# One attention's heads between its projection tiles, and a linear attention in chunk pairs with one scan

## What is computed

```python
a_val, a_gate, q, k, v, b_gate = jnp.split(h @ w_in, EVEN_SPLITS, axis=-1)
q = apply_rope(rmsnorm(to_heads(q, N_Q_HEADS), q_norm_g[li]), cos, sin)   # 6 heads of 128
k = apply_rope(rmsnorm(to_heads(k, N_KV_HEADS), k_norm_g[li]), cos, sin)  # 2 heads of 128
ck = rmsnorm(to_heads(ck, N_KV_HEADS), k_norm_g[li])                      # 256 context tokens
k_all = jnp.concatenate([ck, k], axis=1)
```

## Time and profile before

| | us |
|---|---|
| Runs | 2109.66, 2120.30, 2115.14 |
| Median | 2115.14 |
| The profiled execution's own time | 2111.56 |
| Its span | 2109.7 |
| Its mean granted clock of TensorE | 0.968 |

### The profile page before, as it was taken

How to read it: one execution, slowest core, us unless ns; L and a number is a source line. 1 busy time by engine, 2 the same in 40 slices (tenths; PEclk the granted TensorE clock), 3 DMA queues, 4 the chain that set the end, 5 groups by cost and what they waited for, 6 DMA issues and landing times.

```text
span 2109.7 us, 26132 instructions
## 1 busy us (share of the span) xinstructions
PE 1984.3 (94%) x9634; PEld 1528.7 (72%) x9634; DVE 1165.4 (55%) x1908; ACT 822.2 (39%) x1381; POOL 121.0 (6%) x118
## 2 busy tenths in 40 slices
PE   7997998999799989999999999998999999999997
PEld 5784556788466567776888888775777688888775
DVE  5765756996587686565674234225464574323323
ACT  3424442443422334545543234224445554323321
POOL 0004000000200011000310000000000040000000
PEclk8998899999999999998999999999999899999998
DMA  8583008677001262111212222232211121222222
GB/s 323 189 309 138 0 1 296 239 271 267 16 8 65 95 245 100 41 61 41 81 61 97 95 88 99 80 104 93 83 56 45 41 101 57 94 91 98 99 80 80
DMA packets 46943, 233.38 MB, mean 111 GB/s; under 512 B 5095, under 2 KB 6631, under 8 KB 29832
## 3 DMA queue, kind: packets, MB, share of 16 engines
q1 hardware_dynamic: 46856, 232.22, 30.7%
HBM read 229.97 MB, written 2.10 MB: 110 GB/s over the span
## 4 chain that ended last, share of the span: by engine, by line
PE 80%; DVE 9%; ACT 4%; DMA 3%; issue 2%; POOL 1%; SPq 1%; DVEq 0%; POOLq 0%; ACTq 0%
PE banks L2050 14%; PE banks L2052 14%; PE banks L2051 14%; PE banks L2271 4%; PE banks L2368 3%; PE banks L2370 3%; PE banks L2369 3%; DMA w_raw<-in_wt 2%; PE banks L2291 2%; PE banks L2203 1%; PE banks L2401 1%; PE banks L2214 1%; DVE mod_raw L1278 1%; PE banks L2092 1%; PE banks L2413 1%
## 5 line engine op out<-in xcount | busy, mean ns | idle before, releaser
L1263 DVE TENSOR_TENSOR w_low<-w_raw,w_high 128x1024 fp32r<-128x1024 f32 x184 | 224.8, 1222 | 275.7 <-ACT w_high L506 275.4
L2050 PE MATMUL banks<-h_high,w_high 128*128 128x512 f32 x904 | 352.8, 390 | 7.6 <-DVE w_low L1263 3.9
L2051 PE MATMUL banks<-h_low,w_high 128*128 128x512 f32 x904 | 351.8, 389 | 0.0
L2052 PE MATMUL banks<-h_high,w_low 128*128 128x512 f32 x904 | 351.8, 389 | 0.0
L506 ACT ACTIVATE w_high<-w_raw 128x1024 fp32r<-128x1024 f32 x184 | 193.6, 1053 | 181.9 <-PE banks L2052 140.5
L2050 PE MATMUL banks<-hidden_high,w_high 128*128 128x512 f32 x512 | 207.2, 405 | 0.0
L2050 PEld LDWEIGHTS banks<-h_high,w_high 128*128 128x128 f32 x904 | 169.8, 188 | 46.9 <-issue 9.6
L2052 PE MATMUL banks<-hidden_high,w_low 128*128 128x512 f32 x512 | 200.2, 391 | 0.0
L2051 PE MATMUL banks<-hidden_low,w_high 128*128 128x512 f32 x512 | 200.0, 391 | 0.0
L2052 PEld LDWEIGHTS banks<-h_high,w_low 128*128 128x128 f32 x904 | 169.7, 188 | 35.3
L2051 PEld LDWEIGHTS banks<-h_low,w_high 128*128 128x128 f32 x904 | 169.8, 188 | 34.8
(11 more groups left out here) (495 smaller groups left out, 3551.5 us busy)
## 6 DMA issues: line engine op xcount, KB each, us to landing
w_raw<-in_wt SPq DMA_DIRECT2D x129, 1024.0 KB, 4.9
mod_raw<-in_wmod SPq DMA_DIRECT2D x132, 512.0 KB, 5.0
mod_first<-in_wmod SPq DMA_DIRECT2D x12, 512.0 KB, 14.0
cmp_w<-in_cmp_w SPq DMA_DIRECT2D x2, 2048.0 KB, 8.7
x<-in_xT SPq DMA_DIRECT2D x1, 2048.0 KB, 13.2
dft<-in_dft SPq DMA_DIRECT2D x1, 2048.0 KB, 12.8
out_x<-x SPq DMA_DIRECT2D x8, 256.0 KB, 2.0
hy_w<-in_hy_w SPq DMA_DIRECT2D x8, 192.0 KB, 3.3
```

The lines of the kernel that those rows point to most:

```text
L1263: v.tensor_tensor(low[:, :, :].rearrange("p k c -> p (k c)"), RAW[b // 2][:, b % 2, :], high[:, :, :].rearrange("p k c -> p (k c)").bitcas ...
L2050: mm(out, high[:, k, :], H[:, kk, :], start=start and k == 0, stop=False)
L2051: mm(out, high[:, k, :], L[:, kk, :], start=False, stop=False)
L2052: last = mm(out, low[:, k, :], H[:, kk, :], start=False, stop=stop and k == KT - 1)
```

## The change

**First attention.** The loop over tiles 4 to 19 is written out. `HEADS_AT` says at which tile a head is begun: two at tiles 4 and 5, one at each of 6 to 11. At tile t, ACT takes the root of the heads of tile t-1 and squares those of tile t; PE, after the tile's own 24 matmuls, sums the heads of t and rotates those of t-1; DVE makes the sine part and output of the heads of t-2, then `w_low` of the next tile, then gain and cosine of the heads of t-1, then the tile's units. The heads' sums go to banks 4 and 5 and the rotations to 6 and 7; their buffers are two each. The value transposes stand behind scores 0 and 1. The pool mixer waits for 12 tiles taken and for head 9.

**Linear attention.** Two chunks lie on the two halves of the partitions. So there are 4 groups of transposes, `GA` is 128x4x256 (and the mask is loaded twice), and each chunk's products go to a bank by the chunk's parity. A state's product is four small ones, one for each head, of 32 by 64, so that all states stand in two banks; DVE copies them to `GKV` as [value channel, chunk], and one scan with the decays in `GD` gives all states `GS`, with the chunk innermost. The queries are spread over four buffers `GQ`, one for each head and zero elsewhere (POOL clears them), so that a product reads all 128 rows of `GS`.

**Order behind tile 23.** PE: two groups of transposes, sums of conv, two groups, states, sums of gmlp, results, sums of nsa, the attention's own. ACT and DVE take each group's squares, logarithm, exponential, highs and lows by itself, and `EARLY` has the order conv, gmlp, nsa. The squares of conv move to tile 22; the attention's squares have buffers of their own (`GSQ`). The sums of group 2 stand ahead of tile 3 instead of tile 2, and behind its wait for `w_low`.

```diff
+    GS = at(BIG_AT + 12 * 2 * KB, [P, 64, 8], name="gla_state")
+    GKV = at(BIG_AT + 2 * 2 * KB, [P, 64, 8], name="gla_new")
+    GD = at(BIG_AT + 6 * 2 * KB, [P, 64, 8], name="gla_decays")
+    GA = at(BIG_AT + 19 * 2 * KB, [P, 4, 256], name="gla_att")
+    GQ = [at(BIG_AT + 2 * KB * n, [P, S], name="gla_query") for n in (8, 9, 10, 21)]
+    GSQ = [at(BIG_AT + 2 * KB * n, [P, S], name="gla_sq") for n in (4, 11)]
...
-    BATCHES = (range(0, 4), range(4, NC1))
...
+    HEADS_AT = {4: (0, 1), 5: (2, 3), 6: (4,), 7: (5,), 8: (6,), 9: (7,), 10: (8,), 11: (9,)}
...
+    EARLY, LATE = (0, 1, 6, 7, 2, 3), (4, 5)
...
+    def own_place(c):
+        return slice(64 * (c % 2), 64 * (c % 2) + 64), slice(64 * (c // 2), 64 * (c // 2) + 64)
...
+            if j >= 2:
+                act.wait_ge(taken, (4 + R1[j][1] if R1[j][0] == "q" else R1[j][1]) + 1 + PRIME)
...
+        def head_root(j):
+            rs, n = RSS[j % 2], head_src(j)[1]
+            act.wait_ge(*when(f"hn_ss.{j}"))
+            if j >= 2:
+                act.wait_ge(*when(f"hn_zn.{j - 2}"))
+            nc.scalar.activation(rs[:, 0:n], bank(4 + j % 2, n), ACT.Ln, bias=EPSC[:, :], scale=1.0 / P).then_inc(*did(f"hn_ln.{j}"))
+            act.wait_ge(*when(f"hn_ln.{j}"))
+            nc.scalar.activation(rs[:, 0:n], rs[:, 0:n], ACT.Exp, scale=-0.5).then_inc(*did(f"hn_rs.{j}"))
...
+        for t in range(4, EV_IN):
+            next_tile(t // 4, t % 4)
+            for j in heads_at(t - 1):
+                head_root(j)
+            for j in heads_at(t):
+                head_square(j)
+            copy_out(t // 4, t % 4, z(t), ACT.Copy if t < 12 else ACT.Silu)
+        logs_and_exps()
...
-                nc.scalar.activation(DECY[:, :], GB[:, :].rearrange("p (c t) -> p c t", t=64)[:, :, 63], ACT.Exp, scale=1.0 / 16).then_inc(*did("gla_decay.all"))
+                nc.scalar.activation(GD[:, :, :], GB[:, :].rearrange("p (c t o) -> p o c t", t=64, o=1)[:, :, :, 63].to_broadcast([P, 64, 8]), ACT.Exp, scale=1.0 / 16).then_inc(*did("gla_decay.all"))
...
+                    group_squares(0, ("gm_var.0", "gm_var.1"))
...
             group_squares(3, ("gr_ss.0", "gr_ss.1"))
+            group_log(0)
+            group_root(0)
+            split_high(Q + 6, 1)
             group_squares(1, ("gr_ss.6", "gr_ss.7"))
-            for g in (0, 3, 1):
-                group_log(g)
-            for g in (0, 3, 1):
-                group_root(g)
-            split_high(Q + 6, 1)
-            act.wait_ge(*when("gr_n.3"))
-            for k in range(4):
-                mixed_high(k)
-            for m in range(2):
-                act.wait_ge(*when(f"gla_o.{m}"))
-                nc.scalar.activation(GO[:, m, :], bank(6 + m), ACT.Copy).then_inc(*did(f"gla_out.{m}"))
-                act.wait_ge(*when(f"gr_ss.{2 + m}"))
-                nc.scalar.activation(SQ[m][:, :], bank(6 + m), ACT.Square).then_inc(*did(f"gla_sq.{m}"))
-            for k in (6, 7):
-                mixed_high(k)
+            normal_high(0)
+            normal_high(1)
+            group_log(3)
+            group_root(3)
+            gla_result(0)
+            gla_result(1)
+            group_log(1)
+            group_root(1)
+            normal_high(6)
+            normal_high(7)
             for m in range(2):
...
+            normal_high(2)
+            normal_high(3)
             high_of(Q + 6, 2, KEPT[2][0])
-            group_squares(2, ("gla_ss.0", "gla_ss.1"))
+            group_squares(2, ("gr_ss.2", "gr_ss.3"))
             high_of(Q + 6, 3, KEPT[3][0])
             group_log(2)
             group_root(2)
-            act.wait_ge(*when("gr_n.5"))
             for k in LATE:
-                mixed_high(k)
+                normal_high(k)
...
-        pool.wait_ge(taken, EV_IN + PRIME)
-        pool.wait_ge(*when("in_tabc.all"))
+        pool.wait_ge(taken, 12 + PRIME)
+        pool.wait_ge(*when("hn_out.9"))
...
+                dve.wait_ge(*when(f"hn_zn.{j}"))
+                v.tensor_tensor(RA[j % 2][:, :], ZN[j % 2][:, :], COS0, mul).then_inc(*did(f"hn_ra.{j}"))
...
             dve.wait_ge(*when(f"hn_rot.{j}"))
-            v.tensor_tensor(RB[j % 2][:, :], bank(2 + j % 2), SIN0, mul).then_inc(*did(f"hn_rb.{j}"))
+            v.tensor_tensor(RB[j % 2][:, :], bank(6 + j % 2), SIN0, mul).then_inc(*did(f"hn_rb.{j}"))
             dve.wait_ge(*when(f"hn_rb.{j}"))
             dst = KALL[:, h, CTX:CTX + S] if kind == "k" else z(4 + h)
             v.tensor_tensor(dst, RA[j % 2][:, :], RB[j % 2][:, :], add).then_inc(*did(f"hn_out.{j}"))
...
+        for t in range(4, EV_IN):
+            q, b = t // 4, t % 4
+            if t == 16:
+                dve.wait_ge(*when("silu.row2"))
+                v.tensor_copy(CROW[:, :], CROW2[:, :]).then_inc(*did("next_cond.all"))
+                dve.wait_ge(*when("next_cond.all"))
+            for j in heads_at(t - 2):
+                head_sin(j)
+            next_tile(q, b)
+            for j in heads_at(t - 1):
+                head_norm(j)
+            for j in heads_at(t - 1):
+                head_cos(j)
+            side(q, b, split=False)
...
+                for h in range(4):
+                    rows = slice(32 * h, 32 * h + 32)
+                    v.scalar_tensor_tensor(GQ[h][rows, :], z(11, rows), 32 ** -0.5, GE[3][rows, :], mul, mul).then_inc(*did("gla_m.3" if h == 3 else f"gla_q.{h}"))
...
-                        v.tensor_copy(GS[rows, 1, cols_], bank(4)[rows, cols_]).then_inc(*did(f"gla_st.{c}.{h}"))
+                v.copy_predicated(GA[:, h, :], GMASK[:, 0:256], bank(h, 256)).then_inc(*did(f"gla_att.{h}"))
...
+            dve.wait_ge(*when("gla_kv.3"))
+            v.tensor_copy(GKV[:, :, :].rearrange("p v (j q) -> p q j v", q=2), pair_of_banks(2).rearrange("p q (j v) -> p q j v", v=64)).then_inc(*did("gla_new.all"))
+            dve.wait_ge(*when("gla_new.all"))
+            v.tensor_tensor_scan(GS[:, :, :].rearrange("p v c -> p (v c)"), GD[:, :, :].rearrange("p v c -> p (v c)"),
+                                 GKV[:, :, :].rearrange("p v c -> p (v c)"), 0.0, mul, add).then_inc(*did("gla_st.all"))
...
-            for g in (0, 3, 1):
-                group_norm(g)
+            group_norm(0)
             split_low(Q + 6, 1)
-            dve.wait_ge(*when("gla_o.1"))
-            for k in EARLY:
+            mixed_low(0)
+            mixed_low(1)
+            group_norm(3)
+            group_norm(1)
+            for k in EARLY[2:]:
                 mixed_low(k)
...
-        with led.loop(pe, "ev_in", EV_IN // 4 - 1) as i:
-            for b in range(4):
-                body(i + 1, b, "n0_lo")
...
+            mm(bank(4 + j % 2, n), ONES, SQ[j % 2][:, 0:n], start=True, stop=True).then_inc(*did(f"hn_ss.{j}"))
...
-                mm(bank(2 + j % 2), ROPE0, ZN[j % 2][:, :], start=True, stop=True).then_inc(*did(f"hn_rot.{j}"))
...
+        for t in range(4, EV_IN):
+            body(t // 4, t % 4, None)
+            for j in heads_at(t):
+                head_sum(j)
+            for j in heads_at(t - 1):
                 rot(j)
...
+            if n < 2:
+                pe.wait_ge(taken, EV_IN - 2 + 2 * n + PRIME)
...
+            if n < 2:
+                values_to_tokens(range(3 * n, 3 * n + 3))
...
-            pe.wait_ge(*when("gla_m.2"))
-            for c in range(8):
-                pe.wait_ge(*when(f"gla_tok.{c - 2}" if c >= 2 else "p2t.15"))
-                pe.sem_inc(passed, 1)
-                for m, src in enumerate((GE[2][:, :], z(13), z(14))):
-                    last = nc.tensor.transpose(bank(4 + c % 2)[0:64, m * P:(m + 1) * P], src[:, 64 * c:64 * c + 64], IDENT)
-                last.then_inc(*did(f"gla_tok_mm.{c}"))
...
-            pe.wait_ge(*when("gla_att.3"))
-            for c in range(7):
-                pe.wait_ge(*when("gla_tok.7" if c < 2 else f"gla_st.{c - 2}.3"))
-                mm(bank(4 + c % 2, 256), GV[:, c, 0:P], GV[:, c, P:3 * P], start=True, stop=True).then_inc(*did(f"gla_kv.{c}"))
-                if c:
-                    group_sum((0, 3, 1)[(c - 1) // 2], (c - 1) % 2)
...
+                for m, src in enumerate((GE[2][:, :], z(13), z(14))):
+                    last = nc.tensor.transpose(bank(4 + j % 2)[:, m * P:(m + 1) * P], src[:, P * j:P * j + P], IDENT)
+                last.then_inc(*did(f"gla_tok_mm.{j}"))
...
+                        last = mm(bank(2 + q)[32 * h:32 * h + 32, 64 * j:64 * j + 64], GV[rows, j, 32 * h:32 * h + 32], GV[rows, j, P + 64 * h:P + 64 * h + 64], start=True, stop=True)
+                last.then_inc(*did(f"gla_kv.{j}"))
...
+                    rows, own = own_place(c)
+                    b = 4 + 2 * m + c % 2
...
+                        mm(bank(b)[64 * hp:64 * hp + 64, own], GV[rows, c // 2, P + 64 * h:P + 64 * h + 64], GA[rows, h, own], start=True, stop=c == 0)
                     if c:
-                        last = mm(bank(6 + m)[:, cols_], GS[:, c, P * m:P * m + P], GE[3][:, cols_], start=False, stop=True)
+                        for hp in range(2):
```

(33 more changed lines are left out.)

193 lines of the change are left out of this document (81 added, 112 removed).

## The result

The changed kernel took 2084.01 us (median of 4 runs, 2077.00 to 2087.95), the kernel before 2112.40 beside it: ratio 0.986, 95% interval 0.9837 to 0.9882. It is faster by 28 us at the medians. I had said 2100, with 2088 to 2112 as the range: the direction was right, the size about half. The profiled execution took 2087.95 us, 23.6 less than the 2111.56 of before.

The account below looks back on a forecast made before the run. The prediction took TensorE (PE), busy 94% of the span, as the bound. 17.5 - 2 x 2 = 13.5 us off 2111.56 gave 2098.1, 2101.7 for the median, leaned to 2100 us; range 2088 to 2112.

Parts of the forecast that it names:

- the states of Part B: Linear attention on PE: 32 state matmuls of 64 columns, priced at 4.2 to 6.6 us a layer, taken as 5.0.
- Part B: Linear attention of the two layers: 3.5 us won and 5.6 lost in each, so 2 us slower per layer.
- the stall from POOL: Tiles 13 to 19: the pool mixer beside VectorE makes w_low late, 8 us in sum, bounds 0 and 18.6.
- a head's sums and rotations: Work added to PE between the in-projection tiles: 16 x 1.06 + 2 x 0.62 = 18.2 us.
- the conv sums: Layers, moved before the states: two sums on PE at half clock, 2 x 1.75 = 3.5 us.
- Part A: First attention, heads between in-projection tiles: 25.5 us before stalls, less 8 of stall, gives 17.5 us.
- The tail's term: Layers, from the end of the attention's own sums to the late parts: 17.1 us instead of 11.5.
- (1): In-projection: POOL and VectorE disturb each other little, stall 0 to 2 us, time 2094; chance 0.20.
- (2): Layers: PE keeps its full clock, 5.4 us more gained per layer, time 2091; chance 0.10.
- (3): VectorE becomes the bound: all 18.6 us of POOL fall on PE, layers at half clock, about 2119 at worst; chance 0.10.
- (5): First attention: the interleaving isn't one, as a head's rotation waits on PE for its gain; 2112; chance 0.05.
- (4): Layers' results: weight loads with a 32-byte step cost more, 112 x 0.18 = 20 us if doubled, 2120; chance 0.07.

Follow-up runs that it names:

- e1: The kernel before with only the first attention's part of the change (heads between the tiles): 2089.8 us, 0.9881 of the kernel before.
- e3: The changed kernel with the pool mixer waiting for all 20 tiles, as before the change: 2077.8 us, 0.9824 of the kernel before.
- e2: The kernel before with only the layers' (linear attention) part of the change: 2105.4 us, 0.9955 of the kernel before.
- e7: The changed kernel with the state products reordered, the four groups of one head and partition half following each other: 2090.3 us, 0.9901 of the kernel before.
- e4: The changed kernel with the sums of group 2 ahead of tile 2 again: 2077.0 us, 0.9828 of the kernel before.
- e8: The changed kernel with nsa sums between the results' halves, highs and lows early, group 2 sums ahead of tile 2: 2075.3 us, 0.9827 of the kernel before.
- e10: The changed kernel with the results' state products reading only their head's 32 rows, without the masked query buffers: 2083.1 us, 0.9853 of the kernel before.

## Why the prediction was wrong

The two parts were forecast at 17.5 - 2 x 2 = 13.5 us and gave 31.6 in the profile. Four terms of the sum were priced too high: the states of Part B (5.0 for 1.05, twice), the stall from POOL (8 for 3.8), a head's sums and rotations (18.2 for 14.6) and the conv sums (3.5 for 2.2, twice). Together that is 7.9 + 4.2 + 3.6 + 2.6 = 18.3 us, of the 18.1 that were missed.

**Part A** was forecast at 17.5 us and gave 23.9 in the profile, 25 in e1. Two terms were too large.
- The price of a head's sum or rotation. I took the 1.05 us of a sum between small products; between tiles it is 0.86 (127.40 - 126.54). Sixteen of them and two halves make 14.6 us instead of 18.2: 3.6 us.
- "Sum 8 us", the stall from POOL. It was 3.8, and e3 shows that POOL is its only cause. The step that failed is the walk through the tiles with a whole POOL product of 1.5 us between any two VectorE operations, which lets all 18.6 us of POOL fall on VectorE. The row on which I based it said 1.75 - 0.68 = 1.07 more, and the units beside POOL took 2.30 - 1.22 = 1.08 more, where the product alone takes 5.70 / 4 = 1.43; beside the product of 2.14 they took 2.96 - 1.22 = 1.74 more. Each time it is some 0.4 us less than the product, so a wait for the whole instruction, as the prediction has it, is more than these rows show. The nine units and four `w_low` from 162 to 192 us lost 13.3 us in all. The mechanism was right, the row's own number should have been used. Tile 18 was then 1.4 us late instead of 5.
- The rest: 43.4 - 14.6 - 3.8 = 25.0 less about 1.7 for a clock of 0.76 over the 7.2 us after the waits is 23.3, against 23.9.

**Part B** was forecast at 2 us lost a layer and gained 3.5 and 4.2; e2, with 3.7 and 3.8 on the kernel before, confirms it.
- "States: 5.0" was the worst term: they took 1.05. I had priced them by 64-row, 64-column products; they are 32 columns wide and change places. e7 shows that the order counts; that the width does is read from rows.
- "Conv sums 3.5" at half clock took 2.2, at a granted clock of 0.82 (951.9 to 954.1).
- Results 10.9 (measured 10.5), transposes, nsa sums and own sums were right within 0.7 us. The sum from V to E was 28.8 and came out as 23.8.
- The tail's term held: sums of group 2 at +10.9, late parts at +16.5 for 17.1. e4 confirms the late place of the sums as a part of it; e8, which moves three things at once, agrees with the work ahead of the logarithms as the rest.
- Costing the small edits ahead of V at nothing held: on ScalarE, the lead over the kernel before is 21.1 us at 784 (the time of the kernel before) and still 21.2 at 961, where decays, masks and spread queries lie between.

**The rivals.** (1), little stall, gave 2094 and was nearer for the stall than my forecast; it had 0.20. (2) said full clock in the layers, and that was wrong: 0.72 and 0.62 in results and sums. It had the right time of E for another reason. (3) and (5) did not come. (4) exists at a fifth to a quarter of its price. The range's low end came from taking (1) or (2), never both: 2101.7 - 7 - 10.8 = 2084. They concern different stages and do not exclude each other, so the range should have reached to their sum.

**Open:** where the stretches of lower clock in untouched code come from. No experiment was made on them.

## What to carry to other kernels

When a stage is emptied by moving its work between other matmuls, look at who loses the quiet time: here GpSimd's mixer, which had run where VectorE was busy for 26 of 44 us, cost 3.8 us of waits in its new place, and one changed wait took them away. When groups of work are reordered along a chain, count what stands ahead of the latest result on each engine: that was worth 5 to 7 us a layer here. Price small matmuls by a row with the same columns and the same change of place, and let a range reach to the sum of errors that don't exclude each other.

## What the runs showed of the hardware

**The order of places can halve the time of small matmuls.** Besides e7, the products within chunks show it, with the same operands and in the same bank. Before, all eight chunks went to partitions 0 to 63; after, they alternate between the halves:

```profile
964.20 1.90 PE L2529 MATMUL banks<-gla_e,gla_e 32*64 32x64 f32 x32
```
```profile
943.00 0.97 PE L2568 MATMUL banks<-gla_e,gla_e 32*64 32x64 f32 x32
```

The same 32 records take half the time, both at a granted clock of 1.00. It is not a general rule: the results' products alternate between the output halves too and took 0.065 us a record, and with each head on its own 32 rows as well (e10) the four records with the step still took 0.39 us. No run here separates rows, columns and load time.

**A weight load with a step** of 32 bytes took 208 ns, without 136, for 64 columns; the 8-byte step of the earlier trace rows had 209 for 128 columns. What came through to the path was 0.033 us a load. The note on cachelines in the Trainium skill, SBUF — State Buffer, was right in its direction, and the price here is small.

**GpSimd and VectorE:** a GpSimd product of 1.43 us added 1.08 us to a VectorE pass, one of 2.14 us added 1.74; memsets added nothing.
